# Output projection, first norm and feed-forward end of a decoder layer: four token blocks finished one by one from parked weights

## The reference, cut to what matters

```python
x = layer_norm(x, emb_ln_g, emb_ln_b)                       # 1024 tokens x 1024
proj = x @ w_in                                             # pool, queries, latent, indexer
pool_out, attn_out = ...                                    # pooling; top-256 sparse attention
mix = concat([pool_out, attn_out]) @ w_o                    # 1024 x 1024
x = layer_norm(ALPHA * x + mix, ln1_g, ln1_b)               # ALPHA = 2 ** 0.25
ff = square(relu(x @ w_up)) @ w_down                        # 1024 -> 4096 -> 1024
x = layer_norm(ALPHA * x + ff, ln2_g, ln2_b)
```

## Time and profile before

| | us |
|---|---|
| median of three runs | 1308.09 |
| lowest, highest | 1307.64, 1311.28 |
| span of the profiled execution | 1309.0 |
| PE busy in it | 1223.0 (93%) |
| DVE, ACT, POOL busy | 869.9, 578.9, 539.0 |

### The profile page before, as it was taken

How to read it: one execution, slowest core, us unless ns; L and a number is a source line. 1 busy time by engine, 2 the same in 40 slices (tenths; PEclk the granted TensorE clock), 3 DMA queues, 4 the chain that set the end, 5 groups by cost and what they waited for, 6 DMA issues and landing times.

```text
span 1309.0 us, 17244 instructions
## 1 busy us (share of the span) xinstructions
PE 1223.0 (93%) x5639; PEld 981.3 (75%) x5639; DVE 869.9 (66%) x1322; ACT 578.9 (44%) x961; POOL 539.0 (41%) x390
## 2 busy tenths in 40 slices
PE   4999898799979999999999999989899999999994
PEld 2786685577868778778778698877688888888883
DVE  7577999765879888888888679833842232322345
ACT  3445642675564334243343376642542442433420
POOL 5434674422248666666665733214801102002004
PEclk9899999899989999999999999999799999999997
DMA  6722232131123232332322200403123323223331
GB/s 195 241 74 64 65 81 96 43 119 33 28 70 97 83 101 90 95 96 96 93 87 93 96 1 34 161 17 81 49 98 96 96 96 95 89 90 95 96 96 64
DMA packets 125723, 114.28 MB, mean 87 GB/s; under 512 B 5662, under 2 KB 99435, under 8 KB 125675
## 3 DMA queue, kind: packets, MB, share of 16 engines
q1 hardware_dynamic: 125674, 113.67, 28.0%
HBM read 105.25 MB, written 8.40 MB: 87 GB/s over the span
## 4 chain that ended last, share of the span: by engine, by line
PE 75%; DVE 14%; issue 6%; ACT 2%; POOL 1%; DVEq 1%; DMA 0%; ACTq 0%; POOLq 0%
PE g_bank L1427 14%; PE g_bank L1428 13%; PE g_bank L1429 13%; PE wide L1427 10%; PE wide L1429 10%; PE wide L1428 10%; PE g_bank L1401 2%; DVE logit L924 1%; DVE xlo L563 1%; DVE win L533 1%; PE wide L1530 1%; PE wide L1490 1%; PE wide L1489 1%; DVE probs_lo L940 1%; DVE score L863 1%
## 5 line engine op out<-in xcount | busy, mean ns | idle before, releaser
L397 POOL TENSOR_TENSOR wlo<-wring,whi 128x1024 fp32r<-128x1024 f32 (+1 forms) x102 | 252.4, 2476 | 274.1 <-ACT whi L1133 161.2
L1427 PE MATMUL g_bank<-xhi,whi 128*128 128x512 f32 (+1 forms) x736 | 298.5, 406 | 8.6 <-DVE xlo L563 5.8
L1313 ACT ACTIVATE whi<-wring 128x1024 fp32r<-128x1024 f32 x124 | 131.4, 1059 | 392.9 <-PE wide L1429 198.1
L1428 PE MATMUL g_bank<-xlo,whi 128*128 128x512 f32 (+1 forms) x736 | 294.5, 400 | 0.0
L1429 PE MATMUL g_bank<-xhi,wlo 128*128 128x512 f32 (+1 forms) x736 | 294.2, 400 | 0.0
L397 DVE TENSOR_TENSOR wlo<-wring,whi 128x1024 fp32r<-128x1024 f32 (+1 forms) x70 | 96.6, 1382 | 224.6 <-ACT whi L1313 220.0
L1427 PE MATMUL wide<-whi,hhi 128*128 128x512 f32 x512 | 202.7, 396 | 0.0
L1429 PE MATMUL wide<-whi,hlo 128*128 128x512 f32 x512 | 202.2, 395 | 0.0
L1428 PE MATMUL wide<-wlo,hhi 128*128 128x512 f32 x512 | 202.2, 395 | 0.0
L1427 PEld LDWEIGHTS g_bank<-xhi,whi 128*128 128x128 f32 (+1 forms) x736 | 139.7, 190 | 49.4 <-DVE xlo L563 7.8
L1429 PEld LDWEIGHTS g_bank<-xhi,wlo 128*128 128x128 f32 (+1 forms) x736 | 139.5, 190 | 35.0 <-issue 0.7
(11 more groups left out here) (183 smaller groups left out, 1928.6 us busy)
## 6 DMA issues: line engine op xcount, KB each, us to landing
wring<-in_w_up SPq DMA_DIRECT2D x64, 512.0 KB, 4.2
wring<-in_w_down SPq DMA_DIRECT2D x64, 512.0 KB, 3.5
wring<-in_w_in SPq DMA_DIRECT2D x26, 512.0 KB, 3.9
wring<-in_w_o SPq DMA_DIRECT2D x16, 512.0 KB, 3.5
rows<-in_x SPq DMA_DIRECT2D x8, 512.0 KB, 5.3
normalized_rows<-rows SPq DMA_DIRECT2D x8, 512.0 KB, 4.0
rows<-normalized_rows SPq DMA_DIRECT2D x8, 512.0 KB, 6.6
out<-rows SPq DMA_DIRECT2D x7, 512.0 KB, 2.7
```

What stands on the lines that cost most here:

```text
L397: eng.tensor_tensor(parts_of(name, wlo[n % 2]), parts_of(name, wring[n % 4]), parts_of(name, whi[n % 2]).bitcast(F32), ALU.subtract).then_ ...
L1313: nc.scalar.activation(whi[(first + j) % 2][:, :], wring[(first + j + 2) % 4][:, :], ACT.Copy)\
L1427: nc.tensor.matmul(out_ap, w_hi, m_hi, start=first, stop=False)
L1428: nc.tensor.matmul(out_ap, w_hi, m_lo, start=False, stop=False)
```

## The change

Four things. (1) In both output projections the second half of the columns runs by block: for b, for u. Its four weight units are all kept at once ("parked") in high and low tiles laid over memory that is free by then. (2) DVE applies norm 1 with its gain and bias to the rows of each block as it completes (`x1_norm`), PE transposes rows of two blocks at a time (`x1T` has two halves of four pieces), and ACT and DVE only split what is transposed. `normalized`, `x1_gains` and the ACT and DVE affine steps go. The residual of norm 2 is no longer scaled by ALPHA: the feed-forward sum is scaled by 1/ALPHA in its evacuation, and eps of norm 2 is divided by ALPHA squared. (3) Dots 16 to 47 are moved forward, and in chunk 1 DVE's two first splits of feed-forward units and ACT's `hi` of them move into the projection. (4) The last four down-units of the last group are parked in the place of `xhi` and `xlo` and run by block, and DVE alone does the last norm.

```diff
+        park_at = (40, 44, 64, 68, 72, 76, 88.25, 92.25)
+        wo_hi = [part(f"wo_hi{u}", park_at[2 * u], [P, D], F32R) for u in range(4)]
+        end_hi = [part(f"end_hi{u}", 4 * u, [P, D], F32R) for u in range(4)]
 def projection_steps():
-    return [(nh, u, b) for nh in range(2) for u in range(4) for b in range(CB)]
+    return [(0, u, b) for u in range(4) for b in range(CB)] + [(1, u, b) for b in range(CB) for u in range(4)]
 def dots_after(c, nh, u, b):
+    counts = [1, 2] * 8 + [1] * 8 + [0] * 8
 # DVE
+def x1_norm(c, l, b):
+    dve.wait_ge(gains_in, 32 * (2 if c == 0 else 4))
+    dve.wait_ge(stats_ready, n + 1)
+    chain(scalar_tensor_tensor(out=y, in0=y, scalar=mean, in1=gains[:, 0, :], op0=subtract, op1=mult))
+    dve.wait_ge(rstd_ready, n + 1)
+    scalar_tensor_tensor(out=y, in0=y, scalar=rstd, in1=gains[:, 1, :], op0=mult, op1=add).then_inc(x1_rows, 1)
 def add_residual(c, l):                      # per step with u == 3: add, statistics; with nh == 1 also:
+                            x1_norm(c, l, b)
+                            if b == CB - 2:
+                                x1_lo(dve, c, 0, range(3))
+                    if c and (nh, u, b) in ((0, 3, CB - 1), (1, 0, 0)):
+                        split_lo(dve, ("mlp", 1, nh), lo_dve)
+                x1_lo(dve, c, 0, [3])
+                x1_lo(dve, c, 1, range(4))
-            x1_gains(dve, 0, chain)
 # ACT
+                next_hi = {(0, 0, 3): [("wo", c, 0, 2)], (0, 1, 3): [("wo", c, 0, 3), ("wo", c, 1, 0)],
+                           (0, 2, 1): [("wo", c, 1, 1)], (0, 2, 3): [("wo", c, 1, 2)], (0, 3, 1): [("wo", c, 1, 3)],
+                           (0, 3, 3): [("mlp", c, 0)], (1, 0, 0): [("mlp", c, 1)]}
+                for name in next_hi.get((nh, u, b), []): hi(name)      # ahead of the step's relus
-                normalized(c, l)
-                hi(("mlp", c, 0))
-                hi(("mlp", c, 1))
+                x1_hi(c, 0, range(4))
+                x1_hi(c, 1, range(4))
 # POOL
+            lo(("mlp", 0, 0), ("mlp", 0, 1))
             inverse_std(LN1_0)
-            x1_gains(pool, 1, link)
 # PE
+                    if (nh, u, b) == (1, 1, CB - 1):
+                        x1_transposes(c, 0, range(3))     # waits for the rows of blocks 0 and 1
+                x1_transposes(c, 0, [3])
+                x1_transposes(c, 1, range(4))             # waits for all four blocks
+                if last_group:
+                    for b in range(CB):
+                        for u in range(4):
+                            last = down_products(c, g, 1, b, u, end_hi[u], end_lo[u])
```

More of the change, by code:

```diff
@@ L109, in psum_uses @@
         names += attention(c) + [("proj", c, nh, b) for nh in range(2) for b in range(CB)]
[L110 removed]
+        names += [("x1T", c, half, kp) for half in range(2) for kp in range(KT // 2)]
+        names += [("mlp", c, n) for n in range(GROUPS * GT)]
     return names
@@ L360, in layer, with parked, hi_tile, lo_tile @@
         LO.update({name: (lo_pool, n + 1) for n, name in enumerate(pool_lo)})
+        def parked(name):
+            if name[0] == "wo" and name[2] == 1:
+                return wo_hi[name[3]], wo_lo[name[3]]
+            if name[:2] == ("mlp", 1) and name[2] >= GROUPS * GUNITS - 4:
+                return end_hi[name[2] % 4], end_lo[name[2] % 4]
+            return None
+        ringed = [name for name in units if not parked(name)]
+        R = {name: n for n, name in enumerate(ringed)}
+        def hi_tile(name):
+            return parked(name)[0] if parked(name) else whi[R[name] % 2]
+        def lo_tile(name):
+            return parked(name)[1] if parked(name) else wlo[R[name] % 2]
         def arrivals(n):
@@ L630, in emb_gains @@
                 yield b
-        def x1_gains(eng, c, link):
-            eng.wait_ge(gains_in, 32 * (2 if c == 0 else 4))
-            for n in range(2):
-                link(eng.tensor_scalar(gains[:, n, :], gains[:, n, :], ALPHA, None, ALU.mult))
-            eng.wait_ge(g_full, G[("x1T", c, KT - 1)] + 1)
-            for b in range(CB):
-                link(eng.tensor_tensor(rows[:, b, :], rows[:, b, :], gains[:, 0, :], ALU.mult))
-                eng.tensor_tensor(rows[:, b, :], rows[:, b, :], gains[:, 1, :], ALU.add).then_inc(x1_rows, 1)
         @block.gpsimd
@@ L677, in inverse_std @@
             def inverse_std(l, blocks=range(CB)):
+                eps = EPS / ALPHA ** 2 if l in (LN2_0, LN2_1) else EPS
                 for b in blocks:
@@ L1130, in hi @@
                 act.wait_ge(ring_in[n % 4], arrivals(n))
-                if n >= 2:
-                    wait_product(act, units[n - 2])
-                nc.scalar.activation(parts_of(name, whi[n % 2]), parts_of(name, wring[n % 4]), ACT.Copy).then_inc(hi_ready, 1)
+                if name[0] == "wo" and parked(name):
+                    act.wait_ge(mix_lo_ready, 8 * name[1] + 8)
+                    act.wait_ge(logits_full, 32 * name[1] + 32)
+                elif parked(name):
+                    act.wait_ge(g_full, EV[("mlp", 1, GROUPS * GT - 1)])
+                elif R[name] >= 2:
+                    wait_product(act, ringed[R[name] - 2])
+                nc.scalar.activation(parts_of(name, hi_tile(name)), parts_of(name, wring[n % 4]), ACT.Copy).then_inc(hi_ready, 1)
             def hi_after(name):
@@ L1305, in mlp @@
                             nc.scalar.activation(y_stage[:, b, :], wide[b // 2][:, (b % 2) * 512:(b % 2) * 512 + 512],
-                                                 ACT.Copy).then_inc(y_evac, 1)
-                    if last and c == 1 and j >= GUNITS - 2:
+                                                 ACT.Copy, scale=1.0 / ALPHA).then_inc(y_evac, 1)
+                    if last and c == 1 and j >= GUNITS - 6:
+                        if j < GUNITS - 2:
+                            hi(("mlp", 1, GROUPS * GUNITS - GUNITS + j + 2))
                         continue
@@ L1614, in mlp @@
-            def mlp(c):
+                    h, l = k_pairs(hi_tile(name)), k_pairs(lo_tile(name))
+                    m_hi, m_lo = (pool_hi, pool_lo_part) if u < 2 else (att_hi, att_lo)
+                    acc = bank(("proj", c, nh, b))[:, :]
+                    at = slice(b * P, b * P + P)
+                    if u == 0:
+                        free(("proj", c, nh, b))
+                    for k in range(2):
+                        f = 2 * (u % 2) + k
+                        if nh == 0 and b == 0:
+                            pe.wait_ge(mix_lo_ready, 8 * c + 2 * u + k + 1)
+                        last = three_passes(acc, m_hi[:, f, at], m_lo[:, f, at], h[:, k, :], l[:, k, :],
+                                            u == 0 and k == 0, u == 3 and k == 1)
@@ new lines, in output_projection, with down_products @@
+                    if u == 3:
+                        last.then_inc(proj_full, 1)
+                    elif nh == 0 and b == CB - 1:
+                        last.then_inc(wo_used, 1)
+                    for d in dots_after(c, nh, u, b):
+                        dot(d)
+                    if (nh, u, b) == (1, 1, CB - 1):
+                        x1_transposes(c, 0, range(3))
+                x1_transposes(c, 0, [3])
+                x1_transposes(c, 1, range(4))
+            def down_products(c, g, nh, b, u, slot_hi, slot_lo):
+                h, l = k_pairs(slot_hi), k_pairs(slot_lo)
+                acc = wide[b // 2][:, (b % 2) * 512:(b % 2) * 512 + 512]
+                at = slice(b * P, b * P + P)
+                for k in range(2):
+                    f = 2 * u + k
+                    last = three_passes(acc, hhi[:, f, at], hlo[:, f, at], h[:, k, :], l[:, k, :], f == 0, f == GT - 1)
+                return last
```

284 lines of the change are left out of this document (121 added, 163 removed).

## The result

The changed kernel takes 1297.4 us (median of four runs, 1294.9 to 1300.8) against 1308.0 for the kernel before on the same chip: ratio 0.9906, 95% interval 0.9889 to 0.9923, so 0.94% faster. A second set of runs, against its own runs of the kernel before, gave 1297.3, ratio 0.9906 (0.9889 to 0.9922). The forecast was 1291.7, with 1284.5 to 1299.5 as its range: sign and range hold, and the gain is 11.6 us by the medians in place of 16.4.

What follows compares the result with a forecast made beforehand. TensorE carried 75% of the chain, so time was to be won in its holes after both projections and at the end. Gains 5.3 + 1.6 + 9.5 = 16.4 off 1308.1 gave 1291.7 us, range 1284.5 to 1299.5.

Steps and rivals of the forecast that it cites:

- The end: After the last matmul: only block 3's norm and store remain, span end at 1299.5; gain 9.5 us (8.5 to 10).
- Block price: DVE's chain for one block, add through both norm operations: 4.85 us, against TensorE's 5.6 us per block.
- Chunk 1: Output projection to second feed-forward unit: done at 939.1 against 944.45, gain 5.3 us (bounds 8.8 and 2).
- The late splits: Chunk 1 projection: DVE's two feed-forward weight splits end at 901.2, so DVE starts block 0 5 us late.
- Chunk 0: Output projection to second feed-forward unit: done at 393.0 against 394.65, gain 1.6 us (bounds 4.4 and -3).
- I take 1.5 us of TensorE stall: Chunk 0 projection, first half: stall from full DVE and ACT's stop at `hi` together, 1.5 us (0 to 6).
- a rule of the Trainium skill: Chunk 0: exclusive port lock could cost DVE 14.4 us, not 9.2; 4 us more stall, a 2.5 us loss.
- Feed-forward of chunk 0: The selection lies under this feed-forward, where TensorE is the bound; freeing DVE there was worth nothing.
- The conversion: Span to median: runs' median taken 0.9 us below the 1309.0 span, so 1308.1 less 16.4 gives 1291.7.
- A: Rival: DVE is never late, from early feed-forward copies or a 4.4 us block; 1285.2 us, chance 0.17.
- B: Rival: chunk 0's crowded first half stalls TensorE 6 us or more; 1298.6 us, chance 0.19 shared with another rival.
- C: Rival: ACT's in-order `hi` serializes chunk 0's projection, 28 us of stall; 1318 us, slower than before, chance 0.04.

Runs made afterwards that it cites:

- the repeat of before: The kernel before, run once more without edits: median 1309.3 us, profiled span 1307.0.
- pair 2: Profile comparison: an unedited rerun of the kernel before (span 1307.0 us) against the changed kernel's first profile (span 1292.9).
- pair 1: Profile comparison: the kernel before's first profile (span 1309.0 us) against an unedited rerun of the changed kernel (span 1298.2).
- both late: Changed kernel with chunk 1's two DVE splits and chunk 0's POOL low parts and ACT copies of the first two feed-forward units moved later: ratio 0.9875 to kernel before.

## Why the prediction was right and where it was wrong

**The end** was forecast at 9.5 and is 9.85. Block price 4.85, measured 4.86. The last store is issued 5.1 us after the last matmul, forecast 5.2; from there to the span's end it is 2.6 (1292.9 less 1290.3), taken as 2.8.

**Chunk 1**, forecast 5.3, measured 4.7 and 4.8, went by its steps. Stated from the last `att` (866.85 in the profile that the forecast used, 867.54 in the changed kernel, so 0.69 is to be taken off): DVE's splits end at 901.4, forecast 901.2; transposes of three blocks start at 911.0, forecast 911.1; add of block 3 at 917.4, forecast 918.0; sixteen transposes at 922.3, forecast 922.9; second unit's copy at 938.1, forecast 939.1. By that profile the gain is 6.3. It is 4.8 against the repeat of before, since the 77.6 us of this stretch in the earlier trace rows held 1.6 us of low clock that the repeat (76.1) does not. The late splits, the step's cause, are shown by the experiment that moves them.

**Chunk 0** failed: forecast a gain of 1.6, measured a loss of 1.2 to 3.2. The step that fell is "I take 1.5 us of TensorE stall". Against the repeat of before (both with the high clock at the start), the last projection or dot matmul ends 78.5 us after `att` (375.56 less 2.85, less 294.21) in place of 71.2 (its transposes start at 371.11 after 4.50, `att` at 295.42). Of the 7.3, transposes are 1.5; the stall is 5.8. The rows count 4.1 of it as idle time (67.0 less 62.9), but a stop costs more than that: around the one of 0.48 at 322.28 the starts of matmuls are 0.88 and 0.34 us apart, where 0.23 is usual. Counted by starts the stops are some 4.6 us in the first half of the columns, where the forecast had its 1.5, and 1.8 in the second, where it had no stop at a dot; the steps of the second half win 0.6 back, at 0.227 us a matmul in place of 0.233.

The chain of waits in the rows goes dot, ACT's evacuation, DVE's score, and DVE's score lies beside POOL's low parts. The work on DVE was priced about right, 9.2 us for the six low parts against 9.5 measured. What failed is the step from there to the stall: I had DVE at 39.4 us of 40 and took almost no stall, as if its work could fill every gap. It can't, since a score waits for its dot: DVE idled for 7.2 of the 17.6 us up to 316.6, and then three low parts one behind the other cost it 4.5 us within 7.8. The second half added its share: block 3's add came 2.0 after the last matmul, forecast 1.2. What follows the projection, up to the second unit's copy, was forecast to gain 4.8 and gained 6.1 (27.5 to 21.5) in pair 2 and 4.1 (26.9 to 22.8) in pair 1, the difference being the clock; on the mean that part was right.

I weighed here a rule of the Trainium skill (SBUF — State Buffer, "SBUF: two separate sides") that DVE, in an instruction with two SBUF inputs like the scores, and GpSimd hold their shared port pair exclusively for a whole instruction. By it I had worked out a loss of 2.5 us for chunk 0, at 2.4 us for every low part, and set it aside for the row's 1.5. The trace agrees with a lock: scores beside a low part end about 0.8 us after it (320.51 and 321.32, 323.56 and 324.39), and POOL's part is held in its turn, 3.1 for 2.4. The measured loss of 1.2 to 3.2 lies around the 2.5, but that is luck, since the six low parts cost 1.6 each and not 2.4. No run removes POOL's four `wo` parts from beside the scores, so that they are the cause of most of the 5.8 us is argued from rows, not shown. Shown is that the two `mlp` parts are 1.2 us of it, with ACT's copies 1.8, and that moving the dots out of the second half takes back no more than 2.

**Feed-forward of chunk 0** was priced at nothing, since "TensorE is the bound". It lost 1.2 us, shown by the delayed selection. The mistake is to look at the averages: the change moved DVE's selection against POOL's adds by a few us, and a coincidence that TensorE had escaped now hits it.

**The other feed-forward** gained 0.6 to 0.7, priced at nothing. The kernel with the end by unit has it too (346.6 against 347.2), so it is not the block order of the last group. Its cause stays open.

**The conversion.** The forecast took the profiled span and called the median 0.9 below it. But span and time of one execution differ by about 2 (2.3 here: 1309.0 and 1311.28), and this execution was the slowest of the kernel before, by 3.3 us over the median. Its trace carried low clocks (0.89 at 294 to 310, 0.81 at 927 to 945) that the repeat has less of; the changed kernel's profile happened to be its fastest (1294.91). From profiled execution to profiled execution the gain is 16.4 by their times (16.1 by their spans), exactly the forecast's, and that is luck: like for like it is 10.8 to 14.1, by the medians 11.6.

**The rivals.** A (DVE never late): no, DVE was late in both chunks. B came true in its mechanism and not in its full size: the crowded half has 3.1 us of idle time, 4.6 by the starts, where B said 6 or more, and only with the second half is it 5.8. Its sign, a stall of over 5 us there, did not come; the forecast's own, stops of 1 to 2 us in sum, did not either. Chunk 1 and the end gave more than B said, and its 1298.6 stands 1.2 from the median. The forecast's own 1291.7 is 5.7 from it. C (ACT's order serializes): no; the only wait for a landing that ACT has there is 1.08 us (at 340.36). But the kernel with 12 dots in the second half shows that it is near: there the same copy waits for 3.34.

**The best version** has both late, no dots in the second half, and the selection delayed: 1289.4, ratio 0.9849, some 8 us below the changed kernel and 20 below the kernel before.

## What to carry to other kernels

Before work is moved forward into a stage where TensorE is 100% busy, lay the engine that it lands on against the stage in short stretches, and ask where that engine has to wait for its input: a sum of 39.4 us of work in 40 hid that DVE idled early and was busy for 22.4 of 23.7 us late. POOL's low parts one behind the other cost a DVE that adds scores 2.0 us each here, and themselves 0.7. Finish in the order in which the next engine can take the pieces (block by block, the last one alone behind the last matmul), and keep anything that waits for a transfer out of the way of that chain in its in-order queue. And compare profiles only after their clocks: two profiles of each kernel, cut at common marks, separated a change of 1.2 us from a scatter of 5.

## What the runs showed of the hardware

The clock after a short stop differs between executions of one program. It is seen as the output projections begin (0.89 or 1.00 over 294 to 310, 0.88 or 1.00 over 866 to 880), as the feed-forward of chunk 0 begins (0.65 to 0.92 over 378 to 392), and as the attention of chunk 1 begins, where the following stretch takes 123.2 or 124.5 us. The last, over 15 us from the last copy of the feed-forward, in the kernel with no dots in the second half and then with the selection delayed:

```profile
743.56:758.56 15.00, 12.37 (x66) 8.66 (x63) 10.62 (x25) 10.41 (x23) 11.21 (x12) 1.00 0.00 1
```

```profile
740.92:755.92 15.00, 12.37 (x58) 8.65 (x55) 9.35 (x20) 9.38 (x20) 10.45 (x11) 0.89 0.01 1
```

TensorE has the same two waits in both (1.02 and 1.61 us), and the second loses 1.3 us. A granted clock of 0.89 is a mean: for a part of the stretch the lower of the two levels, 1.2 GHz, was granted, as where the matmuls above start 0.43 apart. What decides between the two cases I could not see in the traces.
